# The third attention of two mixer layers: windows of 8 rows by 16 columns with 256 keys, and a round trip of its values through DRAM

## The chip, the cores and the metric

The kernel runs on one core of one Trainium2 chip. The metric is the device time of one execution in microseconds (us). Five engines work side by side in it: PE (matmul, with its weight loads shown apart as PEld), DVE (vector), ACT (scalar), POOL (GpSimd) and SP, which here only issues DMAs. They meet through semaphores.

## What is computed

512 tokens of width 1024 go through two layers of a first block (feed-forward, mixer, feed-forward) and one layer of a second block (mixer, feed-forward). A mixer has three branches. The change touches one branch of the two mixers of the first block, the neighbourhood attention. The tokens are a grid of 8 rows by 64 columns. Every query sees all 8 rows, and in them only 16 columns around its own:

```python
kr = min(NA_ROW_K, rows)                       # 8 of 8 rows
row_start = jnp.clip(r - kr // 2, 0, rows - kr)
col_start = jnp.clip(c - kc // 2, 0, GRID_W - kc)   # kc = 16, GRID_W = 64
...
scores = jnp.einsum('bhrcd,bhrijd->bhrcij', qg, kg).astype(jnp.float32) * (d ** -0.5)
bias = rpb[:, dr[:, None, :, None], dc[None, :, None, :]]
col_ok = (c[None, :] >= col_start[:, None]) & (c[None, :] < col_start[:, None] + kc)
scores = jnp.where(col_ok[None, None, None, :, None, :], scores + bias, NEG)
p = jax.nn.softmax(...)                        # over the 8 x 64 keys
out = jnp.einsum('bhrcij,bhrijd->bhrcd', p, vg)
```

There are 8 heads of 64 channels. All is float32.

## The kernel before

Activations lie transposed: channels on the 128 partitions, tokens along the free axis (columns X0 = 16 to TW = 528 of each buffer). Every dense product runs as three matmuls (high weights by high data, low by high, high by low), so each weight piece is loaded by SP into `raw` (three buffers, function `pieces`), copied to its high part `wh` by ACT and to its low part `wl` by DVE (function `ahead` of each), and then used by PE. Eight phases v run one after the other; v = 1 and v = 4 are the mixers in question, v = 6 is the mixer of the second block, the rest are feed-forwards.

Each engine has a program of its own, written out in order by Python; `Signal` and `Seat` count the semaphores. A mixer of the first block runs attention C, the dense jobs of B, the branch product of C, attention B, then `q` and `k` of the first pair of heads of A, the values of A, the branch product of B (`merge(v, 1, m)`, m = 0 to 7), attention A, and the branch product of A (`merge(v, 0, m)`), then the output product.

An attention is a list of units (`ATT`), one for each head and block of 128 queries, so 32 for A. In step n the engines do:

- PE (`attention`, `scores`, `turned`, `weighted`): the scores of unit n, some dense filler work (`FILLS`: a quota for each step, one quota being two k-steps of three matmuls), the transposes of unit n - 3 (one of 128 by 128 for each block of keys), and the product of probabilities and values of unit n - 5 (one matmul for each block of keys; in the profile each is two records). For A the quotas are ([2] * 4 + [1] * 4) * 3 + [1, 0] * 4. After the last unit six more steps drain the pipeline.
- DVE (`maximum`, `normalise`, `rest`): adds bias and mask to the scores while taking the maximum (L1889), negates it (L1891), and after the exponentials takes the reciprocal (L1903) and scales (L1907).
- ACT (`exponential`, `turned`, `outputs`): in step n the exponentials of unit n, then weight pieces, the tanh of a gate and stack copies that are due, then the copy of the transposed probabilities of unit n - 3 from PSUM to `PT`. All ACT instructions are on line L1095.
- POOL (`table`): the bias table of a head. Two DMAs of 64 partitions fetch it in runs of 64 floats (L2305, L2307); an addition puts the column mask on it (L2311). The tables of heads 0 and 1 come before the merges of branch 1, that of head x > 1 once the maximum of unit 4(x - 2) + 3 is done.

In A every unit of before takes 128 consecutive tokens (two rows of the grid) as queries and all 512 as keys. `stk` holds high and low parts of queries and keys for a pair of heads; two pairs are in work. `V` holds the values with tokens on the partitions, five tiles of 512; `PT` five tiles of the transposed probabilities. The first tiles of both serve also as gate buffers (`gate_v`, `gate_p`) until the merges of branch 1 have read them. POOL adds up the merges (`macc`, L2294).

Of the kernel before, what the change touches and what calls it, by code (L numbers as in the profile page):

```python
# [44 lines left out]
def consts():  # L45
# [11 lines left out]
    col = np.arange(64)  # L57
    start = np.clip(col - 8, 0, 48)
    ok = (col[None, :] >= start[:, None]) & (col[None, :] < start[:, None] + 16)
    m = np.where(ok, 0.0, NEG).astype(f)  # L60
    c["mask_a"] = np.concatenate([m, m], 0)
# [22 lines left out]
def pack(x):  # L84
# [58 lines left out]
    rp = np.zeros((2, 8, 15, 64, P), f)  # L143
    rp[..., 48:79] = x["na_rpb"][:, :, :, None, :]
    out["rpb"] = rp
# [245 lines left out]
class Units:  # L391
# [11 lines left out]
    "A": Units("A", [(x, j, [1, 2, 3, 4]) for x in range(8) for j in range(1, 5)], 3, 8),  # L403
# [5 lines left out]
def span_of(st, kts):  # L409
    if st == "F":  # L410
        return 0, key_range(kts[-1])[1]
    return key_range(kts[0])[0], key_range(kts[-1])[1]
# [6 lines left out]
def build(nc, T, OUT, CUM):  # L419
    JOBS, PIECES, FILLS = plan()  # L420
    ctx = ExitStack()
    with ctx:
# [51 lines left out]
        maska = sb("maska", [P, 64], F32, XT + 7168)  # L474
# [28 lines left out]
        def gate_buf(v, n, m):  # L503
            if (v < 6 and n == 2) or (v == 6 and n == 0):
                return macc[:, m, :]
            if v < 6:
                return GB[m] if n == 1 else GB[m % 4]
# [26 lines left out]
        def tokens(j):  # L534
            q0 = 0 if j == 0 else X0 + P * (j - 1)
            return slice(q0, q0 + P)

# [69 lines left out]
        class S:  # L607
# [25 lines left out]
            rv = Signal(ctx.enter_context(nc.semaphore("s_rv")))  # L633
            rp = [Signal(ctx.enter_context(nc.semaphore(f"s_rope{i}"))) for i in range(2)]
# [3 lines left out]
                   S.id, S.on, S.lv, S.mt, S.rv, *S.raw, *S.x, *S.o, *S.tab, *S.tb, *S.rp, *S.kd]  # L638
# [21 lines left out]
        def tensor_program(E):  # L660
# [238 lines left out]
            def scores(v, st, n, b, q, ka, kb, done, *events):  # L899

                x, j, kts = ATT[st].units[n]
                k0, k1 = span_of(st, kts)
# [63 lines left out]
            def turned(v, st, u):  # L966
# [3 lines left out]
                buf = u % 3 if st == "C" else u % 4  # L970
# [4 lines left out]
                if 0 in kts:  # L975
# [3 lines left out]
                    i = e.transpose(bank(b0, c0, c0 + P)[0:16, :], tmp[:, buf, 0:16], ident[:, :])  # L979
                    i.then_inc(*S.tp.up(("pt0", v, st, u)))  # L980
                for a in kts:
                    if a > 0:
                        k0, k1 = key_range(a)
                        i = e.transpose(bank(b, P * (a - 1), P * a), tmp[:, buf, k0:k1], ident[:, :])  # L984
                i.then_inc(*S.tp.up(("pt", v, st, u)))

            def weighted(v, st, u):
# [15 lines left out]
                c = slice(P * (j - 1), P * j)  # L1003
                for a in kts:
# [86 lines left out]
        def scalar_program(E):  # L1091
# [169 lines left out]
            def stack(tag):  # L1261
# [9 lines left out]
                for hh in range(2):  # L1271
                    own = slice(64 * hh, 64 * hh + 64)
                    i = act(stk[own, qs[hh] if which == "q" else ks[hh][0], cols], src[own, cols], ACT.Copy)
# [27 lines left out]
            def exponential(v, st, n):  # L1301
# [17 lines left out]
                ee = tmp[:, n % 4, k0:k1]  # L1319
# [6 lines left out]
            def scaled(v, st, n):  # L1326
                x, j, kts = ATT[st].units[n]
                if st == "F":
                    k0, k1 = span_of(st, kts)
                    ee = tmp[:, n % 4, k0:k1]  # L1330
# [3 lines left out]
            def turned(v, st, u):  # L1334
# [13 lines left out]
                a, z = big[0], big[-1] + 1  # L1348
# [920 lines left out]
        def gpsimd_program(E):  # L2269
# [26 lines left out]
            def table(v, x):  # L2296

                if x > 7:
                    return
# [199 lines left out]
```

## Time and profile before

| | us |
|---|---|
| median of 3 runs | 3635.49 (3633.4 to 3637.8) |
| the profiled execution | 3633.74 |
| its span, first to last instruction | 3631.9 |

The span has 1.8 us around it. Engine "busy" is the time in which an engine had at least one instruction in work; matmuls overlap, so the length of one record is not the time from one to the next. The chain of waits is the path of work that ended last; a piece "PE PS L670 x16" is a run of 16 matmul records on that line. Line L984 is the transposes.

### The profile page before, as it was taken

The page shows a single profiled execution, that of the slowest core. Times are in us where ns is not written, and L with a number is a line of the kernel's source. Part 1 is how long each engine was busy: PE and PEld are TensorE (multiplying, and loading weights), DVE is VectorE, ACT ScalarE, POOL GpSimd, SP SyncE. Part 2 cuts the span into 40 slices and gives each one's busy share as a digit, 9 for nine tenths or more (in the row PEclk, how much of TensorE's full clock was granted, in tenths as well). Part 3 has the DMA queues.
Part 4 walks back from the last instruction along what each step waited for, and adds up shares of the span by engine and source line. Part 5 has one row for each costly group of instructions (what it writes and reads, how often), then busy time and mean ns, then how long its engine had stood idle before and what let it go on. Part 6 is the DMA issues. An engine that isn't in the chain of part 4 may idle for free.

```text
span 3631.9 us, 43551 instructions
## 1 busy us (share of the span) xinstructions
PE 3520.3 (97%) x17464; PEld 2932.1 (81%) x17464; DVE 1828.1 (50%) x3164; ACT 1399.9 (39%) x2437; POOL 385.8 (11%) x335
## 2 busy tenths in 40 slices
PE   8999899999999999999899999999999889999998
PEld 6888787888888888888787887888888777878887
DVE  5442565656544335432666575544247565544432
ACT  4222454544432233222454554432236354333221
POOL 0110111122011001100111132011000001201100
PEclk9999999999999999999999999999999999999999
DMA  3223333242232322232423232232322221322232
GB/s 135 98 90 96 101 93 85 66 111 68 77 107 95 93 87 95 97 93 87 110 73 93 73 107 81 74 106 93 92 86 85 84 64 56 102 89 97 95 96 71
DMA packets 107450, 327.07 MB, mean 90 GB/s; under 512 B 15336, under 2 KB 16104, under 8 KB 107248
## 3 DMA queue, kind: packets, MB, share of 16 engines
q1 hardware_dynamic: 98640, 306.89, 27.0%
q0 software_dynamic: 8608, 17.39, 2.6%
q8 instruction: 139, 2.28, 0.3%
q14 instruction: 63, 0.52, 0.0%
HBM read 303.15 MB, written 2.11 MB: 84 GB/s over the span
## 4 chain that ended last, share of the span: by engine, by line
PE 93%; DVE 3%; ACT 2%; issue 1%; DMA 1%; POOL 0%; SPq 0%; DVEq 0%; ACTq 0%
PE PS L670 91%; PE PS L984 2%; ACT wh L1095 1%; DVE wl L1563 0%; DVE stk L1840 0%; DMA raw<-in_gu 0%; DMA tmp<-tmp 0%; DVE tmp L1868 0%; ACT stk L1095 0%; DVE small L1874 0%; DVE ul L1975 0%; ACT tmp L1095 0%; DVE tmp L1872 0%; DVE obl L1931 0%; DVE tmp L1889 0%
## 5 line engine op out<-in xcount | busy, mean ns | idle before, releaser
L670 PE MATMUL PS<-uh,wh 128*128 128x512 f32 (+1 forms) x3336 | 1267.5, 380 | 32.4 <-DVE ul L1591 15.5
L670 PE MATMUL PS<-uh,wl 128*128 128x512 f32 (+1 forms) x3336 | 1262.5, 378 | 0.0
L670 PE MATMUL PS<-ul,wh 128*128 128x512 f32 (+1 forms) x3336 | 1256.2, 377 | 0.0
L1563 DVE TENSOR_TENSOR wl<-raw,wh 128x1024 fp32r<-128x1024 f32 (+2 forms) x595 | 714.3, 1202 | 898.5 <-ACT wh L1095 897.3
L1095 ACT ACTIVATE wh<-raw 128x1024 fp32r<-128x1024 f32 (+2 forms) x595 | 583.9, 984 | 552.4 <-PE PS L670 545.7
L670 PEld LDWEIGHTS PS<-uh,wh 128*128 128x128 f32 x3336 | 630.4, 189 | 162.9 <-DVE gate_p L1970 10.3
L670 PEld LDWEIGHTS PS<-ul,wh 128*128 128x128 f32 x3336 | 631.1, 189 | 120.3
L670 PEld LDWEIGHTS PS<-uh,wl 128*128 128x128 f32 x3336 | 629.9, 189 | 119.1 <-issue 1.4
L670 PE MATMUL PS<-gh,wh 128*128 128x512 f32 (+1 forms) x968 | 363.6, 376 | 0.0
L670 PE MATMUL PS<-gh,wl 128*128 128x512 f32 (+1 forms) x968 | 362.1, 374 | 0.0
L670 PE MATMUL PS<-gl,wh 128*128 128x512 f32 (+1 forms) x968 | 359.7, 372 | 0.0
L2278 POOL TENSOR_TENSOR tmp<-tmp,rb 128x512 f32<-128x512 f32 x110 | 142.5, 1295 | 1370.7 <-ACT tmp L1095 1370.7
L1095 ACT ACTIVATE gh<-tmp 128x512 fp32r<-128x512 f32 x110 | 69.5, 632 | 397.9 <-DVE tmp L1686 397.9
L1095 ACT ACTIVATE tmp<-tmp 128x512 f32<-128x512 f32 (+1 forms) x118 | 74.3, 633 | 376.9 <-DVE tmp L1660 368.1
L1095 ACT ACTIVATE tmp<-tmp,small 128x256 f32<-128x256 f32 (+4 forms) x224 | 134.2, 599 | 221.7 <-DVE small L1891 165.1
L670 PEld LDWEIGHTS PS<-gl,wh 128*128 128x128 f32 x968 | 181.8, 188 | 36.5
L670 PEld LDWEIGHTS PS<-gh,wh 128*128 128x128 f32 x968 | 182.0, 188 | 35.8
L670 PE MATMUL PS<-PT,V 128*128 128x128 f32 x1440 | 201.3, 281 | 9.6 <-DVE obl L1931 8.1
L670 PEld LDWEIGHTS PS<-gh,wl 128*128 128x128 f32 x968 | 181.8, 188 | 33.4
L670 PEld LDWEIGHTS PS<-PT,V 128*128 128x128 f32 x1440 | 182.6, 197 | 12.0 <-DVE obl L1931 10.0
L1686 DVE TENSOR_TENSOR tmp<-PS,tmp 128x512 f32<-128x512 f32 x110 | 76.0, 690 | 170.9 <-PE PS L670 154.8
L2284 POOL DMA_DIRECT2D tmp<-tmp x104 | 82.2, 1282 | 746.5 <-DVE tmp L1825 613.5
(207 smaller groups left out, 3368.3 us busy)
## 6 DMA issues: line engine op xcount, KB each, us to landing
raw<-in_gu SPq DMA_DIRECT2D x220, 512.0 KB, 3.5
raw<-in_win SPq DMA_DIRECT2D x139, 512.0 KB, 3.5
raw<-in_dn SPq DMA_DIRECT2D x80, 512.0 KB, 3.5
raw<-in_wbr SPq DMA_DIRECT2D x72, 256.0 KB, 2.6
raw<-in_dn SPq DMA_DIRECT2D x40, 384.0 KB, 3.1
raw<-in_wout SPq DMA_DIRECT2D x24, 512.0 KB, 3.6
raw<-in_wv SPq DMA_DIRECT2D x20, 512.0 KB, 3.5
stk<-stk SPq DMA_DIRECT2D x72, 128.0 KB, 2.3
```

What stands on the lines that cost most here:

```text
L670: return e.matmul(out, lhs, rhs, start=start, stop=stop, skip_group_check=True)
L984: i = e.transpose(bank(b, P * (a - 1), P * a), tmp[:, buf, k0:k1], ident[:, :])
L1095: return e.activation(out, in_, f, scale=scale, **more)
L1563: tt(wl[:, p % 4, 0:n], raw[:, p % 3, 0:n], wh[:, p % 4, 0:n], SUB).then_inc(*S.lo.up(("lo", p)))
L1686: tt(tmp[:, 2 + f % 2, c0:c0 + cn], bank(job.banks[c], 0, cn), tmp[:, f % 2, c0:c0 + cn], MUL).then_inc(*S.dv.up(("ev", job.tag, c)))
L2278: tt(z, z, rb[:, 0, c0:c0 + cn], MUL).then_inc(*S.pl.up(("z", v, f, c)))
L2284: e.dma_start(tmp[o:o + 32, temp_of(tag), X0:TW], tmp[a:a + 32, turn_of(tag), X0:TW], accum_op=ADD).then_inc(*S.rp[turn_of(tag) == 2].land ...
```

## The change

A unit of A is now a window: 8 rows by 16 columns of the grid as the 128 queries, and 8 rows by 32 columns as 256 keys, which hold every column that these queries may see. `window(j)` gives the first query column, the first key column and which of three bias patterns applies. Heads, units and quotas stay 32, 32 and as they were.

- Queries are put into window order when they are stacked (`by_window` in `stack` on ACT and DVE).
- The scores are two matmuls of 256 columns each, read from the keys as 8 runs of 32 with a step of 64. Two units share one `tmp` row.
- Transposes and weighted products are two instead of four. The weighted product writes 8 runs of 16 floats with a step of 64 into PSUM, so the output is in token order again.
- The values must lie on the partitions in window order. `values_out` writes the four value tiles to a DRAM tensor (4 DMAs of 256 KB), `windows_in` reads the eight tiles of 128 keys back (8 DMAs of 256 KB, source pattern 4 rows by 32 columns by 512 floats) into all of `V` and three tiles of `PT`. Both are on POOL's queue: the first after the tables of heads 0 and 1, the second after the merge of branch 1, m = 3. PE waits for them before its first weighted product.
- A table now comes ready with mask, one DMA of 384 KB; the addition on POOL and the mask's own load are gone.
- The gates 2, 3, 6 and 7 of branch 0 move from `gate_v` and `gate_p` to two rows of `tmp`.

```diff
-    "A": Units("A", [(x, j, [1, 2, 3, 4]) for x in range(8) for j in range(1, 5)], 3, 8),
+    "A": Units("A", [(x, j, [1, 2]) for x in range(8) for j in range(1, 5)], 3, 8),
...
+            return [(0, 0, 0), (16, 8, 1), (32, 24, 1), (48, 32, 2)][j - 1]
...
+            i = 2 * j + r - 2
+            return V[:, i, :] if i < 5 else PT[:, i - 5, :]
...
+                if st == "A":
+                    k0 = window(j)[1]
+                    w = stk[:, q, tokens(j)]
+                    mm(bank(b, 0, 256), w, grid(stk[:, ka, X0:TW])[:, :, k0:k0 + 32], True, False)
+                    i = mm(bank(b, 0, 256), w, grid(stk[:, kb, X0:TW])[:, :, k0:k0 + 32], False, True)
+                    i.then_inc(*done.up(*events))
+                    return
...
+                if st == "A":
+                    E.wait_ge(S.vi, "windows", v)
+                    q = window(j)[0]
+                    out = grid(bank(b))[:, :, q:q + 16]
+                    for r in range(2):
+                        i = mm(out, window_values(j, r)[:, vc], PT[:, 3 + r, c], r == 0, r == 1)
+                    i.then_inc(*S.pv.up((st, v, u)))
+                    return
...
-                e.dma_start(dst[0:64], bass.AP(th, base + 64 * P, [[127, 64], [64 * P, 14], [1, 64]])).then_inc(
-                    *S.tb[x % 2].land(("half", v, x)))
-                e.dma_start(dst[64:128], bass.AP(th, base, [[127, 64], [64 * P, 14], [1, 64]])).then_inc(
-                    *S.tb[x % 2].land(("table", v, x)))
-                E.wait_ge(S.tab[3], "mask", v)
-                E.wait_ge(S.tb[x % 2], "table", v, x)
-                tt(dst, dst, maska[:, :].unsqueeze(1).to_broadcast([P, 14, 64]), ADD).then_inc(*S.pl.up(("tb", v, x)))
+                e.dma_start(tb[:, x % 2, 0:768], T["rpb"][layer_of(v), x]).then_inc(*S.tb[x % 2].land(("table", v, x)))
+
+            def values_out(v):
+
+                for j in range(1, 5):
+                    E.wait_ge(S.aa, "vv", v, "A", j)
+                    e.dma_start(VAL[P * (j - 1):P * j, :], V[:, j, :]).then_inc(*S.vw.land(("values", v)))
+
+            def windows_in(v):
+
+                E.wait_ge(S.vw, "values", v)
+                E.wait_ge(S.pl, "macc", v, 1, 3, 0)
+                for j in range(1, 5):
+                    for r in range(2):
+                        src = bass.AP(VAL.tensor, (256 * r + window(j)[1]) * 512, [[64 * 512, 4], [512, 32], [1, 512]])
+                        e.dma_start(window_values(j, r), src).then_inc(*S.vi.land(("windows", v)))
```

## Rows read from the trace of the kernel before

**Rows 1.** The page, parts 1 and 4: PE's busy time, and the chain by engine
```profile
PE 3520.3 (97%) x17464; PEld 2932.1 (81%) x17464; DVE 1828.1 (50%) x3164; ACT 1399.9 (39%) x2437; POOL 385.8 (11%) x335
...
PE 93%; DVE 3%; ACT 2%; issue 1%; DMA 1%; POOL 0%; SPq 0%; DVEq 0%; ACTq 0%
```

**Rows 2.** Stretch: PE, PEld, DVE, ACT, POOL busy; granted clock; DMA share; GB/s
```profile
763.00:880.00 117.00, 116.12 (x702) 100.62 (x701) 81.82 (x203) 66.27 (x132) 27.27 (x20) 1.00 0.32 85
```

**Rows 3.** Chain of waits, third attention: start us, length us, what, xrecords
```profile
783.14 2.75 PE PS L670 x16
785.89 0.44 PE PS L984 x4
...
789.51 4.14 PE PS L670 x22
...
864.83 1.36 PE PS L670 x10
```

**Rows 4.** Chain of waits, first attention of the second block (256 keys, quota 1)
```profile
2754.14 2.08 PE PS L670 x12
2756.22 0.22 PE PS L984 x2
```

**Rows 5.** Chain of waits, last unit and drain of the third attention
```profile
869.81 1.38 PE PS L670 x10
...
871.21 0.69 DVE tmp L1889
...
873.99 0.58 ACT PT L1095
...
874.70 0.63 PE PS L984 x4
875.33 0.89 PE PS L670 x8
```

**Rows 6.** Waits of PE from 706 to 880 us, all that there are
```profile
PE PS L984 <- ACT PT L1095: 0.9, 1, 0.9
```

**Rows 7.** Groups by form: busy us, mean ns of one, idle before
```profile
L1889 DVE CUSTOM_DVE_ANT_0 tmp<-PS,tb 128x512 f32<-128x512 f32 x64 | 44.1, 689 | 30.0 <-PE PS L670 29.7
L1889 DVE CUSTOM_DVE_ANT_0 tmp<-PS,sbias,par 128x256 f32<-128x256 f32 x24 | 11.5, 478 | 0.3
L1095 ACT ACTIVATE tmp<-tmp,small 128x512 f32<-128x512 f32 x64 | 46.4, 724 | 83.5 <-DVE small L1891 82.8
L1095 ACT ACTIVATE tmp<-tmp,small 128x256 f32<-128x256 f32 x56 | 28.5, 509 | 59.2 <-DVE small L1891 59.2
L1095 ACT ACTIVATE PT<-PS 128x512 f32<-128x512 f32 x104 | 61.1, 589 | 44.3 <-PE PS L984 43.8
L1095 ACT ACTIVATE PT<-PS 128x256 f32<-128x256 f32 x64 | 23.4, 367 | 1.8 <-PE PS L984 1.6
L1095 ACT ACTIVATE stk<-tmp 64x512 fp32r<-64x512 f32 x100 | 62.4, 624 | 12.8 <-DMA tmp<-tmp 10.7 <-issue 1.1 <-DVE tmp L1648 0.3
...
L2352 POOL DMA_DIRECT2D cumb<-cum_d x8 | 4.4, 549 | 114.1 <-DVE tmp L1868 97.6 <-DVE tmp L1872 14.6 <-DMA cum_d<-cumt 1.9
```

**Rows 8.** Timeline: the last value tile of A on ACT
```profile
742.89 0.69 ACT L1095 ACTIVATE V<-PS,small 128x512 f32<-128x512 f32 x1 [0.70 <-PE PS L670]
```

**Rows 9.** Timeline: POOL, merge of branch 1 with m = 3
```profile
754.78 1.80 POOL L2294 TENSOR_TENSOR macc<-macc,gate_p 128x512 f32<-128x512 f32 x1 [0.98 <-DVE gate_p L1970]
```

**Rows 10.** Timeline: PE, scores of the first unit of A
```profile
764.93 0.63 PE L670 MATMUL PS<-stk 128*128 128x512 f32 x2
```

**Rows 11.** DMA: queue (packets, MB, share of 16 engines), issues (KB, us to landing)
```profile
q1 hardware_dynamic: 98640, 306.89, 27.0%
...
tb<-in_rpb POOLq DMA_DIRECT2D x32, 224.0 KB, 4.2
...
cumb<-cum_d POOLq DMA_DIRECT2D x8, 264.0 KB, 3.5
...
out_t<-tmp SPq DMA_DIRECT2D x8, 256.0 KB, 2.1
```

More of the change, by code:

```diff
@@ L141, in pack @@
     ).reshape(1, 512), (P, 512)))
-    rp = np.zeros((2, 8, 15, 64, P), f)
-    rp[..., 48:79] = x["na_rpb"][:, :, :, None, :]
-    out["rpb"] = rp
+    out["rpb"] = np.full((2, 8, P, 768), NEG, f)
+    for t, (q0, k0) in enumerate(((0, 0), (16, 8), (48, 32))):
+        q, k = np.arange(P)[:, None], np.arange(2 * P)[None, :]
+        qc, kc = q0 + q % 16, k0 + k % 32
+        dr, dc = k // 32 - q // 16 + 7, kc - qc + 15
+        start = np.clip(qc - 8, 0, 48)
+        np.copyto(out["rpb"][..., 256 * t:256 * t + 256], x["na_rpb"][:, :, dr, np.clip(dc, 0, 30)],
+                  where=(kc >= start) & (kc < start + 16))
     lw = np.zeros((2, 4, P, P), f)
@@ L506, in gate_buf @@
             if v < 6:
-                return GB[m] if n == 1 else GB[m % 4]
+                return GB[m] if n == 1 else [GB[0], GB[1], tmp[:, 2, :], tmp[:, 3, :]][m % 4]
             return gates[:, m % 2, :]
@@ L1272, in stack @@
                     own = slice(64 * hh, 64 * hh + 64)
-                    i = act(stk[own, qs[hh] if which == "q" else ks[hh][0], cols], src[own, cols], ACT.Copy)
+                    dst, part = stk[own, qs[hh] if which == "q" else ks[hh][0], cols], src[own, cols]
+                    if (st, which) == ("A", "q"):
+                        dst, part = by_window(dst), grid(part).rearrange("p r (w c) -> p w r c", c=16)
+                    i = act(dst, part, ACT.Copy)
                 i.then_inc(*S.aa.up(("cp", tag)))
@@ L1838, in stack @@
                     own, other = slice(64 * hh, 64 * hh + 64), slice(64 - 64 * hh, 128 - 64 * hh)
-                    if which == "q":
+                    if (st, which) == ("A", "q"):
+                        part = grid(src[own, cols]).rearrange("p r (w c) -> p w r c", c=16)
+                        i = tt(by_window(stk[other, qs[hh], cols]), part, by_window(stk[own, qs[hh], cols]), SUB)
+                    elif which == "q":
                         i = tt(stk[other, qs[hh], cols], src[own, cols], stk[own, qs[hh], cols], SUB)
@@ L2328, in mixer @@
                     table(v, x)
+                values_out(v)
                 for m in range(KT):
                     merge(v, 1, m, 2)
+                    if m == 3:
+                        windows_in(v)
                 for x in range(2, 8):
@@ L2429, in sync_program @@
                 E.wait_ge(S.sx, "max", v, "B", 31)
-                e.dma_start(maska[:, :], T["c_mask_a"]).then_inc(*S.tab[3].land(("mask", v)))
                 if v == 4:
@@ L2484, in program @@
     cum = nc.dram_tensor("cum_d", [8, TW], F32, kind="Internal").ap()
-    build(nc, T, out, cum)
+    val = nc.dram_tensor("val_d", [512, 512], F32, kind="Internal").ap()
+    build(nc, T, out, cum, val)
 def kernel(**inputs):
```

53 lines of the change are left out of this document (29 added, 24 removed).

## The prediction

> **What bounds the kernel now.** I read the page first: PE is busy 97% of the span and holds 93% of the chain of waits [rows 1]. Averages hide stages, so I then looked at the third attention (A) of the first layer alone, from 763 to 880 us: PE is busy 116.1 of 117.0 us at a granted clock of 1.00 (its upper level, 2.4 GHz), DVE 81.8, ACT 66.3 and POOL 27.3 [rows 2]. The list of PE's waits from 706 to 880 us has one entry, 0.9 us, on ACT's copy of transposed probabilities [rows 6]. The reader is to see that every microsecond of PE work that leaves this stage leaves the end time, as long as nothing else becomes late, and that DVE at 70% is the next engine. The chain of waits then gives the price of a unit, because it is an even beat there: a run of L670 and a run of transposes (L984). The second layer has the same beat.
>
> **The PE work that goes.** A unit with quota 1 takes 2.75 + 0.44 = 3.19 us; one with quota 2 takes 4.14 + 0.44 = 4.58; one with quota 0 takes 1.36 + 0.44 = 1.80 [rows 3]. So a quota costs 1.39 us, and 1.80 us are attention: four transposes 0.44 (0.11 each), eight records of weighted product 0.89 [rows 5], and the rest, 0.47, two score matmuls of 512. The new unit needs no guess from scratch: the first attention of the second block has just this shape, 256 keys, two transposes, four records of weighted product and quota 1. Its unit takes 2.08 + 0.22 = 2.30 us, 2.29 for most of its neighbours; I use 2.30 less the rounding, 2.29 [rows 4]. The difference to 3.19 is 0.90 us: 0.22 transposes, about 0.45 weighted product, about 0.23 scores. The quotas do not change, so it is the same 0.90 at quota 0 and 2. 32 units times 0.90 is 28.8 us in each of the two layers.
>
> **What comes back in the drain.** After the last unit there is no filler. From the end of the last scores (871.2) to the transposes of unit 30 (874.70) the chain runs over the maximum, the exponentials, a weight piece, a gate's tanh and the PT copy, 3.5 us, while PE has two steps of transposes and weighted product, 2.7 us, and waits 0.9 [rows 5, 6]. After: the maximum falls from 0.69 to 0.48, the exponentials from 0.72 to 0.51 and the copy from 0.59 to 0.37 (the same operations at 256 columns) [rows 7], so the chain is about 2.9 us, but PE's cover is 2 x (0.22 + 0.45) = 1.35. The wait is then about 1.6 instead of 0.9: 0.7 us given back in each layer.
>
> **The units before it.** Transposes of unit m - 1 need the bank that ACT copies out after the exponentials of unit m. The time that PE has for it from the end of scores m is two steps of transposes and weighted product (1.35), two scores (0.44), and one or two quotas in the last eight units: 3.2 or 4.6 us. The chain is the one of the drain: 2.9 us with a weight piece and a tanh in it, and less in the steps without [rows 5, 7]. It just fits, unless DVE is still at a weight piece when the scores come; I take 0.2 us a layer for it. At quota 1 and 2 there is more room, and DVE's and ACT's work in a unit falls as well.
>
> **The DMAs of the values.** The last value tile is copied at 743.6 [rows 8]; writing 256 KB to DRAM takes about 2 us (the output's DMAs of that size, 2.1) [rows 11], so the values are out by 747. `windows_in` waits for more than that: for POOL's merge with m = 3, which ends at 756.6 [rows 9]. Eight issues at 0.55 us (the reload of `cumb` from DRAM, 264 KB in 128 rows) [rows 7] end at 761. Bytes: 2.10 MB. The hardware queue moved 306.89 MB with 27.0% of 16 engines over 3631.9 us, 19.6 GB/s for each engine while busy; with 16 engines and the 32% that weights take here [rows 2, 11], 2.10 MB need about 10 us, so they land near 769. PE needs them in step 5 of A: A's first scores are at 764.9 [rows 10], and before the first weighted product stand six scores (1.3), quotas 2, 2, 2, 2, 1, 1 (13.9) and three units of transposes (0.7), so 780.8. The cover is 12 us; the cost is nothing. Behind `windows_in` in POOL's queue stand the merges m = 4 to 7, and after them the table of head 2. Merge 4 would start at 761 instead of 757.6, but each merge takes 1.3 to 1.8 us and its data come every 2.8 to 3 us, so POOL has caught up at merge 7, near 767. Who waits for that merge is the stack copy of the second pair, which comes in step 3, near 777.
>
> **Tables.** POOL loses 16 additions, 16 DMA issues and the mask. The load is one of 384 KB in long rows instead of two of 224 KB in runs of 256 bytes that landed in 4.2 us; the nearest row for long rows is 264 KB in 3.5 [rows 11], so 3.5 to 4.5. The tightest is the last: from the maximum of unit 23 to unit 28 there are four units at a mean of 1.6 us, 6.4, against issue and landing of 4 to 5. Cover 1.4 to 2.4 us, cost nothing, at worst 1 us a layer. That POOL's additions no longer disturb DVE gains nothing, since PE waited for DVE nowhere here.
>
> **Strided operands.** The trace of before has no matmul that reads its moving data in 8 runs of 32 or writes 8 runs of 16 into PSUM. Below, the cost is zero, since the count of columns is what 512 against 256 columns and the 128-column records pay for [rows 3, 4]; a gain has no reason. Above, I bound it by twice the time of the six records. I take zero, because nearest are the contiguous rows and every run is still 16 or more floats long. The stack copies of queries get runs of 16 floats; contiguous they take 0.62 us [rows 7], and even doubled they lie two units ahead of their use.
>
> The Trainium skill (SBUF — State Buffer, section "Door 1: The DMA port swizzle") says that PSUM has lines of 8 bytes and that any non-contiguous PSUM pattern slows matmuls significantly. Read literally it speaks against this output pattern; no row of before tests it. It stands as a rival below.
>
> **Sum.** 2 x (28.8 - 0.7 - 0.2) = 55.8 us less. The profiled execution took 3633.7, so 3577.9; against the median of 3635.5 that is 3579.7. I give 3580.
>
> **Rivals.**
>
> 1. The softmax chain becomes the limit in the last eight units (alternating quotas 1 and 0): they keep their old mean of 2.49 us. Against it stands the count above, which fits without room; for it, that DVE and ACT run in order and a job's copies fall between. Price 8 x 0.90 = 7.2 a layer, so 3594. Chance 0.08.
> 2. The windows land late. Their source pattern has an outermost dimension of 4. If this keeps each DMA on four engines, and all on the same four, those move 524 KB each: 26.8 us alone at 19.6 GB/s, 39 with the weights' 32% beside it [rows 2, 11]. They would land at 786 to 798, and PE, which needs them at 780.8, would stand 5 to 17 us a layer. Time 3590 to 3614, middle 3602. Against it: nothing in the rows shows any DMA confined so. Chance 0.06. The Trainium skill (DMA: Bandwidth & Descriptors, section "Why a DMA increments its semaphore by 16 and not by 1") says that the number of engines is the largest up to 16 that divides the slowest dimension of both patterns, here 4, but that DMAs issued from GpSimd take consecutive engines from a cursor that moves on. By that rule the eight DMAs go round all 16 engines and the landing stays near 769; only without the cursor does the rival hold.
> 3. Strided access costs PE some speed: scores and weighted product take twice their new time, 0.23 + 0.45 = 0.68 us a unit, 43.5 us over 64 units, so 3623; with the weighted product alone, 0.45 x 64 = 29, so 3609. Chance 0.08. This is what the page's rule on PSUM lines would come to here.
> 4. Slower than before: the same mechanism, stronger. From 0.90 us of extra time a unit on, the change loses; over the four weighted records of about 0.11 us each, that is 0.225 more for each, three times the contiguous time. At four times for them and twice for the scores the extra is 1.35 + 0.23 = 1.58 a unit, 0.68 net, 44 us over 64 units: 3679. Nothing in the rows speaks for it except that the pattern is untried. Chance 0.04.
> 5. The forecast itself, all others excluded: 0.74, its own range 3572 to 3588.
>
> **How the numbers follow.** The time is that of case 5. The range takes in cases 5 and 1 (0.82) and the low half of 2: 3572 to 3600. The low end is the full 57.6 us, some 3 us for an error of 0.05 in the unit price and 2 for the spread of the runs. This kernel's measurement can tell about 0.2%, 7 us, from no change. Faster by more than that: cases 1, 2, 3, 5, less a little for a stronger form of 3 that lands close to zero: 0.95. Within: 0.01. Slower: 0.04.
>
> **What would show it.** In A the chain should beat with 2.07 + 0.22 us at quota 1, 3.46 + 0.22 at quota 2 and 0.68 + 0.22 at quota 0; weighted records and scores should start at the old distances for their column counts (0.11 and 0.11 us). PE's waits should show one of about 1.6 us in the drain on ACT's PT copy and none on the DMAs of `V` and `PT`; a wait there before the first weighted product is rival 2. A beat above 2.4 us at quota 1 is rival 3 or 4, by the distance between records. Waits of PE on ACT or DVE in the last eight units are rival 1. The rest of the span, the feed-forwards and attentions B and C, should keep its times; the prediction is wrong if the stages beside A move.

## The result, and the profile of the changed kernel

| | before | after |
|---|---|---|
| median, device us | 3634.4 (3632.4 to 3637.8, 4 runs) | 3587.9 (3585.1 to 3590.1, 4 runs) |
| ratio | | 0.9871, interval 0.9854 to 0.9888 |
| profiled execution: time, span | 3633.7, 3631.9 | 3585.1, 3583.3 |

The kernel is 46.5 us faster. The forecast was a saving of 55.8 us and a time of 3580, with 3572 to 3600 as the range: sign and range held, and the size was 9 us too large. The page of after, its busy times, its chain by engine and its two DMA queues, against [rows 1] and the queue row of [rows 11]:

```profile
span 3583.3 us, 42774 instructions
...
PE 3462.6 (97%) x17080; PEld 2879.5 (80%) x17080; DVE 1789.0 (50%) x3164; ACT 1372.9 (38%) x2437; POOL 346.5 (10%) x327
...
q1 hardware_dynamic: 98352, 306.82, 27.8%
q0 software_dynamic: 12320, 22.66, 3.1%
...
PE 91%; DVE 4%; ACT 2%; DMA 2%; issue 1%; POOL 0%; SPq 0%; DVEq 0%; ACTq 0%; POOLq 0%
```

PE has 57.7 us less work (3520.3 to 3462.6), as planned, but its share of the chain fell from 93% to 91% and DMA's rose from 1% to 2%. The hardware queue moves the same bytes and takes 27.8% of the engines instead of 27.0%. So the place to look is where DMAs and A meet. The chain of after, around the start of A in the first layer:

```profile
758.78 22.69 DMA PT<-val_d
...
781.51 4.21 PE PS L696 x12
```

One of the eight reads of `windows_in` takes 22.69 us, and PE stands until it is there. The beat behind it is the forecast one. The chain again, a step with quota 2, one with quota 1, one with quota 0, and the drain (L696 is the old L670, L1018 the old L984, L1137 the old L1095, L1938 the old L1889):

```profile
792.56 3.49 PE PS L696 x18
796.05 0.22 PE PS L1018 x2
...
805.96 2.09 PE PS L696 x12
808.05 0.22 PE PS L1018 x2
...
842.37 0.69 PE PS L696 x6
843.06 0.22 PE PS L1018 x2
...
849.52 0.42 DVE tmp L1938
...
852.37 0.41 PE PS L1018 x2
```

PE's waits from 690 to 870 us, where before had the one of [rows 6] in the drain (after has 1.6 there) and another of 1.9 us before 706, which is in after too (us in total, times, longest):

```profile
PE PS L1018 <- ACT PT L1137: 3.4, 2, 1.9
PE PS L696 <- DMA PT<-val_d: 3.4, 1, 3.4
```

The stage can be measured by two starts in the PE timeline: from the first scores of A to the first product of the branch behind it. In before these are at 764.93 [rows 10] and here:

```profile
879.10 0.48 PE L670 MATMUL PS<-obh,wh 128*128 128x512 f32 x1
```

So A takes 114.17 us. In after:

```profile
761.93 0.40 PE L696 MATMUL PS<-stk 128*128 128x256 f32 x2
...
854.54 0.47 PE L696 MATMUL PS<-obh,wh 128*128 128x512 f32 x1
```

That is 92.61 us, a saving of 21.6 where the forecast had 27.9. The second layer gives 114.16 and 92.89. These lengths of A repeat to about 0.1 us between kernels that have no collision, while medians scatter by 2 to 4 us, so they are the yardstick of the experiments.

The distances between the starts of successive scores (31 in each layer; here the first nine, then the mean of those with quota 2, 1 and 0) tell where in A it is. E9 is a kernel of batch 3 below, whose reads are quick.

| us | first nine steps | quota 2 | quota 1 | quota 0 |
|---|---|---|---|---|
| before | 3.25 3.25 3.26 3.60 2.30 3.20 3.19 3.18 4.58 | 4.58 | 3.19 | 1.80 |
| after | 3.02 3.03 3.03 3.16 1.85 **6.37 4.26** 2.42 3.69 | 3.69 | 2.30 | 0.91 |
| E9 | 3.02 3.02 3.02 3.17 1.86 2.30 2.30 2.86 3.67 | 3.69 | 2.30 | 0.91 |

The loss against E9 is in steps six and seven, 6.0 us of which step eight gives back 0.4: the wait for the values (3.4 us, 778.1 to 781.5) and a slow stretch behind it. Stretches of after (PE, PEld, DVE, ACT, POOL busy; granted clock; DMA share; GB/s):

```profile
760.00:765.00 5.00, 5.00 (x25) 4.07 (x24) 2.73 (x6) 1.08 (x3) 5.00 (x4) 1.00 1.04 188
765.00:770.00 5.00, 5.00 (x25) 4.16 (x24) 1.67 (x5) 1.06 (x1) 0.50 (x1) 1.00 1.05 222
...
775.00:780.00 5.00, 3.12 (x17) 2.34 (x15) 3.44 (x13) 2.99 (x8) 0.59 (x1) 1.00 0.99 255
780.00:785.00 5.00, 3.49 (x11) 3.10 (x12) 3.00 (x8) 3.09 (x7) 0.00 (x0) 0.51 1.00 207
```

Two things stand there. All 16 DMA engines are busy (a share of about 1) while only some 190 to 255 GB/s move; and after PE's stall the granted clock is 0.51, its lower level of 1.2 GHz, so that matmuls of 512 columns start 0.43 us apart instead of 0.23, until about 787. Last, the DMA issues (KB each, median us from issue to landing), first of the whole span, then of 750 to 785 us:

```profile
V<-val_d POOLq DMA_DIRECT2D x10, 256.0 KB, 9.2
...
val_d<-V POOLq DMA_DIRECT2D x8, 256.0 KB, 2.5
...
PT<-val_d POOLq DMA_DIRECT2D x6, 256.0 KB, 18.1
```

```profile
raw<-in_win SPq DMA_DIRECT2D x8, 512.0 KB, 10.8
stk<-stk SPq DMA_DIRECT2D x4, 128.0 KB, 4.6
```

Not only are the reads late (9.2 and 18.1 us). The weight pieces on SP's queue, 3.5 us over the whole span and 3.5 in before's 750 to 785, take 10.8 beside them, and the halves of the stacks, `stk<-stk`, 4.6 instead of 2.4. In the second layer the loss comes along these, as its chain shows:

```profile
2072.87 10.97 DMA raw<-in_win
...
2096.11 8.33 DMA stk<-stk
```

PE waits in that A 3.0 us for the stack and 1.0 for `PT`, and the clock is 0.66 in the 5 us after 2104.

### The profile page after: what moved, and what is told of

The parts are those of the page before. It is cut to its first block, busy times and chain, and to the rows that moved or that the text cites. A ratio compares the mean times of both kernels' runs of the same rounds, so it can differ in the third digit from the quotient of the medians.

```text
span 3583.3 us, 42774 instructions
## 1 busy us (share of the span) xinstructions
PE 3462.6 (97%) x17080; PEld 2879.5 (80%) x17080; DVE 1789.0 (50%) x3164; ACT 1372.9 (38%) x2437; POOL 346.5 (10%) x327
## 3 DMA queue, kind: packets, MB, share of 16 engines
q1 hardware_dynamic: 98352, 306.82, 27.8%
q0 software_dynamic: 12320, 22.66, 3.1%
q8 instruction: 136, 2.23, 0.3%
## 4 chain that ended last, share of the span: by engine, by line
PE 91%; DVE 4%; ACT 2%; DMA 2%; issue 1%; POOL 0%; SPq 0%; DVEq 0%; ACTq 0%; POOLq 0%
PE PS L696 89%; PE PS L1018 1%; ACT wh L1137 1%; DMA PT<-val_d 1%; DVE wl L1609 1%; DVE stk L1889 0%; DMA raw<-in_gu 0%; DMA raw<-in_win 0%; ACT stk L1137 0%; DMA tmp<-tmp 0%; DVE tmp L1917 0%; DMA stk<-stk 0%; DVE tmp L1938 0%; ACT tmp L1137 0%; DVE small L1923 0%
## 5 line engine op out<-in xcount | busy, mean ns | idle before, releaser
L696 PE MATMUL PS<-uh,wh 128*128 128x512 f32 (+1 forms) x3336 | 1267.0, 380 | 31.5 <-DVE ul L1637 14.6
L696 PE MATMUL PS<-uh,wl 128*128 128x512 f32 (+1 forms) x3336 | 1261.9, 378 | 0.0
L696 PE MATMUL PS<-ul,wh 128*128 128x512 f32 (+1 forms) x3336 | 1255.9, 376 | 0.0
L1137 ACT ACTIVATE wh<-raw 128x1024 fp32r<-128x1024 f32 (+2 forms) x595 | 583.8, 984 | 559.7 <-PE PS L696 545.9
L696 PEld LDWEIGHTS PS<-uh,wh 128*128 128x128 f32 x3336 | 630.5, 189 | 159.2 <-DVE tmp L2019 10.3
L696 PEld LDWEIGHTS PS<-ul,wh 128*128 128x128 f32 x3336 | 630.6, 189 | 119.9
L696 PEld LDWEIGHTS PS<-uh,wl 128*128 128x128 f32 x3336 | 629.9, 189 | 116.8 <-issue 1.4
L696 PE MATMUL PS<-gh,wh 128*128 128x512 f32 (+1 forms) x968 | 363.6, 376 | 0.0
L696 PE MATMUL PS<-gh,wl 128*128 128x512 f32 (+1 forms) x968 | 362.1, 374 | 0.0
L696 PE MATMUL PS<-gl,wh 128*128 128x512 f32 (+1 forms) x968 | 359.6, 372 | 0.0
L1137 ACT ACTIVATE gh<-tmp 128x512 fp32r<-128x512 f32 x110 | 69.5, 632 | 398.0 <-DVE tmp L1732 398.0
L1137 ACT ACTIVATE tmp<-tmp 128x512 f32<-128x512 f32 (+1 forms) x118 | 74.3, 633 | 377.0 <-DVE tmp L1706 368.1
L696 PEld LDWEIGHTS PS<-gl,wh 128*128 128x128 f32 x968 | 181.8, 188 | 36.5
L696 PEld LDWEIGHTS PS<-gh,wh 128*128 128x128 f32 x968 | 182.0, 188 | 35.8
L696 PEld LDWEIGHTS PS<-gh,wl 128*128 128x128 f32 x968 | 181.8, 188 | 33.4
L1137 ACT ACTIVATE tmp<-tmp,small 128x256 f32<-128x256 f32 (+3 forms) x224 | 120.4, 538 | 195.3 <-DVE small L1940 139.2
L696 PE MATMUL PS<-PT,V 128*128 128x128 f32 x1088 | 157.6, 280 | 14.5 <-DVE obl L1980 8.6
L1706 DVE TENSOR_TENSOR tmp<-PS,rb 128x512 f32<-128x512 f32 x110 | 75.9, 690 | 169.3 <-PE PS L696 169.3
```

The costliest lines, as they stand in the source:

```text
L696: return e.matmul(out, lhs, rhs, start=start, stop=stop, skip_group_check=True)
L1137: return e.activation(out, in_, f, scale=scale, **more)
L1706: i = tt(tmp[:, tag[2] % 2, c0:c0 + cn], ps, r, MUL)
```

## Experiments

In each the base is the kernel after; "A" is the length of the stage in the first and the second layer, measured as above (before 114.17 and 114.16; after 92.61 and 92.89). Medians of one batch share their runs of the kernel before. E1, E2, E4, E6, E7 and E8 attend to values (E8 also to keys) that are not the window's, so what comes out of them is not the attention asked for.

### Batch 1: do the reads cost the missing part, and why are they slow?

**E1, no reads.**

```diff
-                    E.wait_ge(S.vi, "windows", v)
...
-                        i = mm(out, window_values(j, r)[:, vc], PT[:, 3 + r, c], r == 0, r == 1)
+                        i = mm(out, V[:, 1 + (2 * j + r - 2) % 4, vc], PT[:, 3 + r, c], r == 0, r == 1)
...
-                E.wait_ge(S.pl, "macc", v, 1, 3, 0)
...
-                        e.dma_start(window_values(j, r), src).then_inc(*S.vi.land(("windows", v)))
```

> The changed kernel without the eight reads of the windows; the products take value tiles that are there already, so the output of this attention is not the reference's. The values are still written to DRAM. Theory 1 (all that is missing against the forecast is the late landing of the windows and what hangs on it: waits, late weight pieces, the granted clock after them): about 3580 against 3588, no wait of PE in the first six steps, clock 1.00 through the stage. Rival (the missing 8 us are elsewhere, in the drain or in strided operands): stays at 3586 to 3588.

Measured: 3581.0 (3578.5 to 3583.9), ratio 0.9857 [0.9842, 0.9872]; A 86.94 and 86.97. PE's waits from 700 to 870:

```profile
PE PS L1018 <- ACT PT L1136: 3.4, 2, 1.8
PE PS L696 <- DVE small L1937: 0.3, 1, 0.3
```

The wait for the values is gone and 5.7 and 5.9 us of A with it. The reads cost that; the rest of the change brings 27.2 us a layer.

**E2, as many bytes from 128 rows in a line.** The two reads of a window take the same rows here.

```diff
-src = bass.AP(VAL.tensor, (256 * r + window(j)[1]) * 512, [[64 * 512, 4], [512, 32], [1, 512]])
+src = bass.AP(VAL.tensor, 128 * (j - 1) * 512, [[512, 128], [1, 512]])
```

> The changed kernel with a source of 128 rows in one run instead of 4 times 32 rows, same bytes, same place in the queue; other rows than the reference's are fetched. Theory 1 (the DMA engines are shared between two queues and the volume sets the landing): last landing still 18 us or more after its issue, time 3585 to 3588. Rival 2 (an outermost dimension of 4 keeps each transfer on four engines, which makes it late): the first landing falls from 9 us to about 4, the last one to about 10, and the time falls to about 3580.

Measured: 3580.7 (3579.7 to 3583.1), ratio 0.9855 [0.9838, 0.9871]; A 86.95 and 86.95, the same as with no reads at all. Its software queue and the landings in `PT` (those in `V` take 4.3 us), and then the stretch that in after moved 222 GB/s:

```profile
q0 software_dynamic: 9248, 22.64, 2.8%
...
PT<-val_d POOLq DMA_DIRECT2D x6, 256.0 KB, 6.4
```

```profile
765.00:770.00 5.00, 5.00 (x26) 4.12 (x25) 3.02 (x6) 1.55 (x3) 4.54 (x3) 1.00 0.97 381
```

So 2.10 MB in this place cost nothing. What costs is the pattern in which they are read. The same busy engines move 381 GB/s. The queue has 3072 packets fewer than in after, of the kind described under E7.

**E3, six of the eight reads early**, as soon as the values are in DRAM; the two into tiles that are in use until then stay behind the merge m = 3.

```diff
+                        if (2 * j + r - 2 in (0, 5)) == late:
...
+                windows_in(v, False)
...
-                        windows_in(v)
+                        windows_in(v, True)
```

> The changed kernel, full computation, with six of the eight reads issued as soon as the values are in DRAM (about 12 us earlier) and only the two tiles that share memory with gate buffers after the fourth merge. If the start is what is too late: all land before 770, no wait of PE on them, time about 3580. If the volume beside the weights is what hurts, weight pieces come late in the merges of branch 1 instead: 3583 to 3588.

Measured: 3590.1 (3588.9 to 3591.3), ratio 0.9882 [0.9867, 0.9896]; A 93.89 and 94.02. It is no better than after, although no wait of PE for the values is left. The collision has moved, into the pieces of weights that ACT and DVE prepare just before A and in its first steps (timeline of ACT, then a stretch):

```profile
761.05 1.06 ACT L1137 ACTIVATE wh<-raw 128x1024 fp32r<-128x1024 f32 x1 [7.14 <-DMA raw<-in_win]
```

```profile
770.00:775.00 5.00, 1.70 (x9) 1.18 (x8) 2.32 (x5) 2.25 (x4) 2.09 (x2) 1.00 0.93 239
```

ACT stands 7.14 us for a weight piece, and 4.4 for the next; DVE's low parts and, behind them in its program, a maximum come late, and PE waits 3.3 us for that maximum and is busy 1.70 of 5 us. The second step of A takes 6.48 us (E9: 3.02). The expected 3580 was missed by 10 us, and so was 3583 to 3588 for late weights. That was the lesson of the batch for me: the wait on the values is only one of the ways in which these reads cost.

**E4, the same pattern from another tensor**, one that nobody writes (`wbr`, an input).

```diff
-src = bass.AP(VAL.tensor, ...
+src = bass.AP(T["wbr"].tensor, ...
```

> The changed kernel with the same eight reads, same pattern, but from an input tensor (branch weights) instead of the freshly written values; the output is not the reference's. If reading back what was just written, or that one region of DRAM, is slow: landings fall to 4 to 10 us and the time to about 3580. If not: landings of 9 and 18 us and 3586 to 3588 as before.

Measured: 3587.5 (3586.5 to 3588.3), ratio 0.9874 [0.986, 0.9889]; A 92.71 and 91.63.

```profile
PT<-in_wbr POOLq DMA_DIRECT2D x6, 256.0 KB, 17.3
```

The landings are nearly those of after (the reads into `V` take 9.2 us). That the source was just written has no part in it, and another place in DRAM did not help either.

### Batch 2: the pattern's outermost dimension

**E6 and E7, sixteen runs of 8 rows and eight runs of 16 rows** instead of four runs of 32.

```diff
-[[64 * 512, 4], [512, 32], [1, 512]]
+[[12 * 512, 16], [512, 8], [1, 512]]
```

and in E7, of the same line:

```diff
-[[64 * 512, 4], [512, 32], [1, 512]]
+[[24 * 512, 8], [512, 16], [1, 512]]
```

> The changed kernel with the values read as 16 runs of 8 rows with gaps between them (same bytes; other rows than the reference's). If the outermost dimension sets how many of the 16 engines carry a transfer, this is like the contiguous source: landings of 4 and 6 us, about 3580.5. If gaps in the source are what slows it: 9 and 18 us, about 3587.

> The changed kernel with the values read as 8 runs of 16 rows with gaps (same bytes; other rows than the reference's). By the count of engines this lies between: two transfers in work instead of four fill all 16 engines, each transfer some 6 to 7 us, the last about 12, time 3581 to 3584. By gaps alone it would be like 4 and 16 runs alike.

Measured: E6 3581.8 (3578.7 to 3583.2), ratio 0.9853 [0.9837, 0.987], A 87.20 and 87.24; E7 3579.8 (3577.6 to 3586.4), ratio 0.9853 [0.9838, 0.9868], A 88.41 and 87.53. E7's median lies 1 us below the 3581 to 3584 expected, and its four runs are 9 us apart, so its A is the better measure. E6 and then E7:

```profile
q0 software_dynamic: 9248, 22.64, 2.8%
...
PT<-val_d POOLq DMA_DIRECT2D x6, 256.0 KB, 8.2
```

```profile
q0 software_dynamic: 10272, 22.65, 2.9%
...
PT<-val_d POOLq DMA_DIRECT2D x6, 256.0 KB, 12.2
```

The landings (in `V` and in `PT`) go by the outermost dimension: 4 gives 9.2 and 18.1 us, 8 gives 7.0 and 12.2, 16 gives 4.6 and 8.2, 128 gives 4.3 and 6.4. What A loses against E1 goes with them: 5.7 and 5.9 us at 4, 1.5 and 0.6 at 8, 0.3 at 16 (which a slow operation of DVE, told under E11, may have caused as well), nothing at 128. Rows that are scattered cost little in themselves, since sixteen runs are more scattered than four. The packets say how the work is spread. Each read has 64 data packets of 4096 bytes in every kernel. Beyond these there are, with 16 reads in a program, (12320 - 9248) / 16 = 192 packets of 8 bytes more in each read of after, and (10272 - 9248) / 16 = 64 more in E7. That is 12 engines of 16 packets, and 8 engines of 8: each engine without data gets as many tiny packets as the others get data. So, by the counts, one read lies on 4, on 8 or on 16 engines. This is the rule of the Trainium skill (DMA: Bandwidth & Descriptors, section "Why a DMA increments its semaphore by 16 and not by 1"): the largest number up to 16 that divides the outermost dimension of both patterns. The counts agree with it. What it says of a cursor, by which successive reads go on round the engines, agrees too: in after, from 761 to 766 us, the packets of the reads alone take 68.2% of the time of 16 engines, and four engines are 25%.

```profile
q0 software_dynamic: 406, 0.59, 68.2%
```

What neither the Trainium skill's rule nor the forecast had is the third thing in the trace: the 4096-byte packets of the reads, taken one by one, take 306 ns (median in the first layer) with four runs, 281 with eight, 230 with sixteen, and 159 in a line. The packets of the other queue slow down beside them (median 331 ns from 761 to 766 us in after, 159 from 760 to 765 in E2). With twice the time for each packet, 16 busy engines move about half the bytes, and whatever else is in flight on them waits.

**Why** a packet takes longer is open. It isn't the scatter alone: E5 and E9 below read the very rows of after, in another order, at 159 ns. It isn't the number of engines alone either: E6 has 16 engines by its counts, like E2 and E9, and takes 230 ns, and the quarters of E11, each a plain run of rows, take 253. E2, E6 and E9 have the same number of engines and differ only in which rows of DRAM are read and in which order, so the places in DRAM count for something. With four engines each of them also has 32 of the 128 partitions to write where one of sixteen has 8, and no run separates that from the rest.

**E5, the keys of a window in column order**: 32 columns by 4 rows, so that the same read has 32 outermost. The scores, the table and the two copies that fill the stacks of k are reordered with it.

```diff
-src = bass.AP(VAL.tensor, (256 * r + window(j)[1]) * 512, [[64 * 512, 4], [512, 32], [1, 512]])
+src = bass.AP(VAL.tensor, (256 * r + window(j)[1]) * 512, [[512, 32], [64 * 512, 4], [1, 512]])
...
-mm(bank(b, 0, 256), w, grid(stk[:, ka, X0:TW])[:, :, k0:k0 + 32], True, False)
+part = [stk[:, k, X0:TW].rearrange("p (r k) -> p r k", r=2)[:, :, 4 * k0:4 * k0 + P] for k in (ka, kb)]
+mm(bank(b, 0, 256), w, part[0], True, False)
...
+                    elif st == "A":
+                        dst, part = by_column(dst), by_row(part)
...
+                        i = tt(by_column(stk[own, ks[hh][1], cols]), by_row(src[own, cols]),
+                               by_column(stk[own, ks[hh][0], cols]), SUB)
```

> The changed kernel, full computation, with the 128 keys of a tile in another order: 32 columns outside, 4 rows inside. The read of a value tile then is 32 runs by 4 rows by 512 floats, outermost dimension 32 instead of 4; keys are stacked in that order, and the scores read two runs of 128 columns. If the outermost dimension of 4 is what makes the reads late: landings of 4 to 7 us, no wait on them, about 3580, 8 us under the changed kernel. If it is that the rows are not one contiguous run: landings of 9 and 18 us and 3587. The stack copies of the keys may slow down (0.62 us each before); at twice that they still hide.

Measured: 3586.9 (3584.8 to 3588.9), ratio 0.987 [0.9855, 0.9884]; A 89.99 and 89.89. The reads into `PT` (those into `V` land in 4.4 us), and the group of the reordered copies on DVE (busy us, mean ns | idle before):

```profile
PT<-val_d POOLq DMA_DIRECT2D x6, 256.0 KB, 6.0
```

```profile
L1902 DVE TENSOR_TENSOR stk<-tmp,stk 64x512 fp32r<-64x512 f32 x16 | 17.5, 1092 | 14.2 <-ACT stk L1146 14.1
```

The landing is cured, and about half of the gain in A is given back elsewhere: 3.1 us a layer against E9. A copy that writes single floats 16 bytes apart takes 1092 ns on DVE instead of the 686 of the copies that are not reordered, and some 1.1 us on ACT instead of 0.62. A's steps wait for them: steps seven, eight and sixteen take 3.00, 3.96 and 3.39 us (E9: 2.30, 2.86 and 2.29), and PE waits 1.6 us for DVE. The expectation that copies of twice the time would still hide, and with it the 3580, failed.

**E8, plain operands**: each read takes 128 rows in a line, from eight different places, and scores and weighted product read and write in one piece.

```diff
-mm(bank(b, 0, 256), w, grid(stk[:, ka, X0:TW])[:, :, k0:k0 + 32], True, False)
+mm(bank(b, 0, 256), w, stk[:, ka, X0 + k0:X0 + k0 + 256], True, False)
...
-out = grid(bank(b))[:, :, q:q + 16]
+out = bank(b, 8 * q, 8 * q + 128)
```

> The changed kernel with contiguous source for the values and contiguous operands on PE: scores read 256 columns in one run, the weighted product writes 128 columns in one run (keys, values and places of the output are not the reference's). If the runs of 32 and of 16 floats cost PE nothing: equal to the contiguous source alone, 3580.7 within its spread, and the same beat of 2.30 us at quota 1. If they cost: less by 64 times the difference of the beat.

Measured: 3578.9 (3574.7 to 3582.3), ratio 0.9847 [0.9832, 0.9862]; A 86.87 and 86.88. Beside E2's 86.95 the strided operands cost 0.08 us in 32 units. The beat is 2.08 + 0.22 in E8, and the steps at quota 1 take 2.29 to 2.30 in both. That eight different sources do as well as E2's four also clears E2 of the rows that it reads twice. The medians, 1.8 us apart, overlap.

### Batch 3: versions that keep the gain

**E9, order the keys once.** As E5, but the permutation is made where k is taken out of PSUM, in four operations of 128 partitions a layer, and all stack copies are contiguous again.

```diff
+                    elif kind == "k" and tag[2] == "A":
+                        i = tt(by_column(tmp[:, temp_of(tag), c0:c0 + cn]), by_row(ps), by_row(r), MUL)
```

> Full computation, keys in column order as in the run with columns outside, but the new order is written once, when DVE takes the keys out of PSUM, so that the two ACT and two DVE stack copies of each pair are contiguous again. If those copies (0.99 to 1.13 us instead of 0.62 and 0.69, on the way to the scores in steps 2 to 6 and 10 to 14) ate the gain: about 3580. If something else of the column order did (the scores' two runs, the table): stays at 3587.

Measured: 3580.9 (3579.7 to 3582.2), ratio 0.9853 [0.9839, 0.9868]; A 86.91 and 86.92. It leaves nothing out and beats both kernels: all its runs lie below all those of after. The reads into `PT` (those into `V` land in 4.3 us), the one slow operation (from 700 to 860), and PE's waits from 2000 to 2200, around the second layer's A:

```profile
PT<-val_d POOLq DMA_DIRECT2D x6, 256.0 KB, 6.1
```

```profile
L1705 DVE TENSOR_TENSOR tmp<-PS,rb 128x512 f32<-128x512 f32 x4 | 4.4, 1089 | 3.2 <-PE PS L704 3.2
```

```profile
PE PS L1027 <- ACT PT L1146: 3.4, 2, 1.8
PE PS L704 <- DVE small L1949: 0.3, 1, 0.3
```

The waits for DMA are gone in both layers, and the strided write costs 0.4 us four times, at a place where PE doesn't wait for it. A is as long as with no reads at all.

**E10, E9 with the filler moved into the drain**: one quota is taken from step 24 (23 in the expectation, which counts from 0), and one put behind the last scores.

```diff
-([2] * 4 + [1] * 4) * 3 + [1, 0] * 4
+([2] * 4 + [1] * 4) * 2 + [2] * 4 + [1] * 3 + [0] + [1, 0] * 4 + [0, 1]
```

> The run before, with one quota of filler of A moved from step 23 to step 33, in the drain, where PE waits 1.6 us for ACT's copy of the transposed probabilities. If that wait is an uncovered latency: 1.4 us less in each layer, about 3577. If ACT's queue only gets later by it (the gate's tanh moves behind): same as the run before.

Measured: 3580.4 (3578.0 to 3582.1), ratio 0.9851 [0.9837, 0.9866]; A 86.23 and 86.19. PE's waits from 700 to 870:

```profile
PE PS L1027 <- ACT PT L1146: 1.8, 1, 1.8
PE PS L704 <- DVE small L1949: 0.3, 1, 0.3
...
```

(The 1.8 us are the wait before A that before and after have too.) The wait of 1.6 us in the drain is 0.3, and the stage is 0.7 us shorter, not the 1.4 that were expected: two more waits of 0.3 have come, and one step near the end takes 1.35 us where E9 has 0.90. Two times 0.7 us is less than a comparison of medians can tell.

**E11, four DMAs for each read**, 32 partitions each, each a plain run of rows.

```diff
-                        e.dma_start(window_values(j, r), src).then_inc(*S.vi.land(("windows", v)))
+                        for i in range(4):
+                            t = 256 * r + 64 * i + window(j)[1]
+                            e.dma_start(window_values(j, r)[32 * i:32 * i + 32], VAL[t:t + 32, :]).then_inc(
+                                *S.vi.land(("windows", v)))
```

> The changed kernel, full computation, with each read of a value tile split into four DMAs of 32 partitions with a contiguous source of 32 rows (32 DMAs of 64 KB instead of 8 of 256 KB). All 16 engines carry each; the price is POOL's issue, 32 times 0.55 to 0.65 us, 18 to 21 us from 754 on, so the last lands near 775, before the first product (778), but the merges 4 to 7 wait behind it until then and with them the stack copy of the second pair. Expected 3580 to 3585; if small DMAs from POOL are cheaper than 0.5 us to issue, 3580.

Measured: 3585.0 (3583.3 to 3586.8), ratio 0.9866 [0.9849, 0.9882]; A 91.14 and 91.08. POOL's timeline, and then DVE's:

```profile
756.12 9.79 POOL L2365 DMA_DIRECT2D V<-val_d  x20 [0.56 <-POOL macc L2343]
765.90 5.86 POOL L2365 DMA_DIRECT2D PT<-val_d  x12
771.78 5.11 POOL L2343 TENSOR_TENSOR macc<-macc,stkf 128x512 f32<-128x512 f32 x4
```

```profile
771.13 4.62 DVE L1956 TENSOR_SCALAR tmp<-tmp,small 128x256 f32<-128x256 f32 x1
```

The quarters land in 3.8 and 4.1 us, but 32 issues at 0.49 us hold POOL's queue for 15.7 us, and the merges behind them end at 776.9 instead of 765.5. A's steps five to eight take 2.23, 3.87, 3.37 and 3.96 us, with 1.5 us of waits for DVE and 1.3 for ACT. The trace puts them down to something that nobody expected: one scaling operation of DVE takes 4.62 us instead of 0.35 (4.58 at 2085.0 in the second layer), the next maximum waits behind it in DVE's program, and ACT stands 5.93 us for that one. These 4.3 us are about what A loses against E1, 4.2 and 4.1. In the other changed kernels no operation of this form takes over 0.47 us. It starts during POOL's last issues and ends during the merges; E6 has the like of it at the same point, a low part of a weight piece that takes 4.30 us instead of 1.23 at 761.0, where it costs A little. What holds DVE there is not shown. Whether the merges, which end 11 us later than in after, would have cost anything by themselves stays open, since ACT's stack copies stand behind the late maximum anyway.

## Why the prediction was right, and where it was off

**Units (right).** The forecast beat was 2.07, 3.46 and 0.68 with 0.22 of transposes; measured 2.08 or 2.09, 3.46 to 3.49 and 0.69 with 0.22. The price taken from another attention of the same shape [rows 4] was good to 0.01 us at quota 1. The steps save 0.89 us each instead of 0.90.

**Drain (right).** Forecast a wait of 1.6 us; in after and in E9 it is 1.56, and the chain from the last maximum to the transposes takes 2.85 us (849.52 to 852.37) where 2.9 was said. The maximum took 0.42 (forecast 0.48, from a form with other operands).

**Tables (right).** The one DMA of 384 KB lands in 3.6 us in the median (3.5 to 4.5 said; one beside the reads of the first layer took 10.4), and no wait of PE goes back to a table.

**The units before the drain (right), but not the ones at the start.** The last eight units have no wait (rival 1 is dead: their mean is 1.60 us, the two quotas together 3.20, not 2 x 2.49). The forecast allowed 0.2 us a layer for them. What came instead is one late step at the start, the eighth, 2.86 instead of 2.29, with the wait of 0.3 us for DVE that E1, E2, E8 and E9 all show. That is 0.6 us a layer.

**Sum without the reads.** E9's A saves 27.26 and 27.24 us, together 54.5, where the sum had 55.8; the 1.3 us are the late step (0.6 in place of 0.2) and 0.01 in each of some 26 steps, twice. Medians of the kernels whose reads do little harm (E1, E2, E6, E8, E9) are 52.1 to 55.3 us below before's of their batch, which fits.

**The DMAs of the values (wrong): the step that failed.** It read "so they land near 769. [...] The cover is 12 us; the cost is nothing." What stands around the landing was near enough: the write took 2.5 us (2 said); the issues began at 754.15, behind the merge, and ended near 759.4, 0.66 us each (0.55 said); PE needed the values at 778.1, where 780.8 less the 3 us by which this execution reached A earlier is 777.8. Only the landing was 781.5. The term was 2.10 MB over 16 engines at 19.6 GB/s each beside the weights. That speed is the average of the weights' queue, carried over to a pattern with 4 outermost; the packets show 4096 bytes in 306 ns, 13 GB/s an engine, and all 16 engines stayed full for 20 us. Cost: 5.7 us in the first layer and 6.0 in the second (A of after less A of E9), 11.7 in all. So the forecast from before's 3634.4, 3578.6, misses the measured 3587.9 by 9.3 = 1.3 (A without the reads) + 11.7 (the reads) - 3.7.

**The 3.7 us outside A, and luck.** I can't place these 3.7 us for certain. In the profiled executions after is shorter than before by 3.0 us ahead of the first A, 0.4 between the two, and 2.4 behind the second; but E9 reaches the first A at 764.93, just as before does, and the twelve changed kernels, whose programs are alike behind the second A, take from 1411.8 (after) to 1417.3 us there (before 1414.2). So a good part is scatter of executions, and no stage beside A is shown to have moved. It need not be all: by the same reckoning the five kernels with a costly collision (after, E3, E4, E7, E11) lie 1.7 to 3.7 us below what their A says, and of the other seven six lie 0.6 to 2.3 above and one (E8) 0.7 below. In any case 3587.9 lies just inside the forecast's own range, 3572 to 3588, by grace of these 3.7 us; what was understood adds up to 3591.6. The range up to 3600 had been opened for rivals 1 and 2. That the size came out within 9 us is in part luck.

**What the step left unpriced.** Of the 5.7 us in the first layer only 3.4 are the wait. The rest is the lower clock from 781.5 to about 787, some 2.6 us, less the 0.4 that step eight gives back; PE has no further wait there. In the second layer the wait on the values is just 1.0 of the 6.0 us, and 3.0 are a wait for a stack whose DMA took 8.33 us instead of 2.4. I had asked whether the transfer comes in time for its own user. I had not asked what it does to the others in flight, and E3 shows that this alone can cost as much.

**Rival 2, at 0.06, was half the truth.** It had the cause (outermost dimension 4, four engines each), the place and the sign; it assumed "all on the same four", and priced 3590 to 3614. The counts say four engines each, and the trace shows all sixteen busy. The Trainium skill's rule had been set against it ("By that rule the eight DMAs go round all 16 engines and the landing stays near 769"): its premises hold, and the conclusion, which was mine, does not follow, since engines that are all busy can still be slow. "Nothing in the rows shows any DMA confined so" was true, and was no evidence, as none of those rows had so small an outermost dimension.

**Rivals 3 and 4 (dead).** E8 against E2 bounds all strided operands of PE together at 0.1 us a layer. The Trainium skill (SBUF — State Buffer, section "Door 1: The DMA port swizzle") says that any non-contiguous PSUM pattern slows matmuls significantly; here, with runs of 16 floats, it doesn't. The bound "twice", from having no row, cost chance (0.12) but not the forecast. For copies a price would have been in place: single floats 16 bytes apart cost DVE 1.6 times and ACT about 1.8 times (E5).

## What to carry to other kernels

Look at the outermost dimension of both patterns of every new DMA before its bytes: a duration is best borrowed from a row with the same one, and 32 could be had here, with the same rows, by reordering what is moved, at the one place where the data is written anyway (E9), not at every copy (E5) nor by more issues (E11). Ask of a new transfer not only whether it is in time, but which loads of other queues are in flight with it and who stands when those take two or three times as long. When PE stalls, count the stretch at the lower clock behind the stall as well.

## What the runs showed of the hardware

- A read of 256 KB whose source has 4, 8, 16, 32 or 128 outermost, issued eight at a time beside weights, lands in 9.2 and 18.1, 7.0 and 12.2, 4.6 and 8.2, 4.3 and 6.1, 4.3 and 6.4 us (medians of the first five, to `V`, and of the last three, to `PT`).
- Beside its 64 data packets such a read has 192 packets of 8 bytes at 4 outermost, 64 at 8, and none at 16 or more: as many for each engine without data as the others have data packets.
- Its data packets of 4096 bytes take 306, 281, 230, 159 and 159 ns, at the same size and number, and 253 ns when each read is split into four of 32 partitions. Why is open.
- Beside the slow reads a 512 KB load on the other queue takes 10.8 us instead of 3.5, and a 128 KB copy within SBUF up to 8.3 instead of 2.4.
- Around the end of a stall of 3.4 us TensorE's granted clock was 0.51 (780 to 785), and 0.66 in the 5 us around and after the end of the second layer's, of 3.0 us; with no stall it was 1.00 in the same place (E2: 780 to 785).
- A DMA of 32 partitions costs POOL 0.49 us to issue, one of 128 partitions 0.54 to 0.66 on average: what is issued is nearly as dear when it is a quarter.
- With 32 DMAs issued in a row by POOL, one operation of DVE on 256 columns took 4.62 and 4.58 us in the two layers, instead of 0.35; in E6 one took 4.30 instead of 1.23 behind 8 issues. What holds DVE is not shown.
